# Modulation blocks accumulated on VectorE in the first FFN's loop, and an input projection begun with four feature tiles per chunk of tokens

## What is computed

```
mod = silu(c) @ w_mod + b_mod            # sh1,sc1,g1, sh2,sc2,g2, sh3,sc3,g3
h = rmsnorm(x, ng[0]) * (1 + sc1) + sh1
x = x + g1 * 0.5 * swiglu(h, gate0, up0, down0)        # FFN width 2816
h = rmsnorm(x, ng[1]) * (1 + sc2) + sh2
proj = h @ w_in                          # 2560 columns: q, k, v, xr, xg
o  = differential attention(q, k, v)     # 4 heads
rg = bidirectional RG-LRU(conv(xr)) * gelu(xg)
x = x + g2 * (concat(o, rg) @ w_out)
h = rmsnorm(x, ng[2]) * (1 + sc3) + sh3
x = x + g3 * 0.5 * swiglu(h, gate1, up1, down1)
y = rmsnorm(x, final_g)
```

## Time and profile before

| what | value |
|---|---|
| runs of the kernel before | 2498.46, 2496.99, 2494.31 us; median 2496.99 |
| the profiled execution | 2498.43 us, span 2496.6 us |
| granted TensorE clock, mean over the span | 0.978 of full speed |
| PE, PEld, DVE, ACT, POOL busy | 2396.6, 2236.1, 1128.3, 668.6, 29.7 us |
| DMA | 144.52 MB, mean 58 GB/s |

### The profile page before, as it was taken

One profiled execution on the slowest core, in us unless ns is written; L12 is line 12 of the kernel. 1 busy time (PEld: TensorE's weight loads), 2 busy tenths in 40 slices (PEclk: granted clock), 3 DMA queues, 4 the chain that ended last, 5 costly groups with the idle time before them and its releaser, 6 DMA issues.

```text
span 2496.6 us, 35528 instructions
## 1 busy us (share of the span) xinstructions
PE 2396.6 (96%) x14392; PEld 2236.1 (90%) x14392; DVE 1128.3 (45%) x1845; ACT 668.6 (27%) x1174; POOL 29.7 (1%) x36
## 2 busy tenths in 40 slices
PE   5999999999999998999989988999999999999997
PEld 3799999999999987777977768979999999999996
DVE  3544333443334436465557773364443344443335
ACT  3411111111111124465236663251111111111112
POOL 0000000000000000000010030000000000000000
PEclk8999999999999999999989999999999999999998
DMA  9222022210222103111100010111101110101102
GB/s 372 85 75 77 18 83 84 77 74 20 81 84 82 44 1 119 34 34 41 43 21 20 29 46 18 59 52 34 50 22 46 50 50 34 49 22 46 50 9 77
DMA packets 45817, 144.52 MB, mean 58 GB/s; under 512 B 5808, under 2 KB 13360, under 8 KB 45744
## 3 DMA queue, kind: packets, MB, share of 16 engines
q1 hardware_dynamic: 45744, 143.49, 16.7%
HBM read 133.50 MB, written 9.97 MB: 57 GB/s over the span
## 4 chain that ended last, share of the span: by engine, by line
PE 90%; DVE 4%; ACT 3%; DMA 1%; issue 1%; SPq 0%; ACTq 0%; DVEq 0%
PE ps L433 27%; PE ps L435 26%; PE ps L434 26%; PE ps L679 4%; PE ps L708 2%; PE ps L632 2%; DVE sb_tmp L1191 1%; PE ps L694 1%; DVE sb_hL L1183 1%; PE ps L460 1%; DMA sb_stage<-in_w_mod 1%; ACT sb_pr L1036 1%; PE ps L445 1%; PE ps L453 0%; PE ps L470 0%
## 5 line engine op out<-in xcount | busy, mean ns | idle before, releaser
L433 PE MATMUL ps<-sb_hH,sb_guH 128*128 128x384 f32 x2112 | 716.2, 339 | 9.8 <-DVE sb_hL L1183 6.3
L435 PE MATMUL ps<-sb_hH,sb_guL 128*128 128x384 f32 x2112 | 708.0, 335 | 0.0
L434 PE MATMUL ps<-sb_hL,sb_guH 128*128 128x384 f32 x2112 | 708.0, 335 | 0.0
L433 PEld LDWEIGHTS ps<-sb_hH,sb_guH 128*128 128x128 f32 x2112 | 398.0, 188 | 33.7 <-issue 17.4
L1255 DVE SCALAR_TENSOR_TENSOR sb_x<-ps,sb_mod,sb_x 128x128 f32<-128x128 f32 (+1 forms) x704 | 345.9, 515 | 180.9 <-PE ps L435 178.7
L434 PEld LDWEIGHTS ps<-sb_hL,sb_guH 128*128 128x128 f32 x2112 | 398.4, 189 | 0.7 <-issue 0.3
L435 PEld LDWEIGHTS ps<-sb_hH,sb_guL 128*128 128x128 f32 x2112 | 398.3, 189 | 0.0
L1242 DVE TENSOR_TENSOR sb_tmp<-ps,sb_tmp 128x384 f32<-128x384 f32 x132 | 73.5, 557 | 670.6 <-PE ps L435 669.3
L433 PE MATMUL ps<-sb_hidH,sb_dnH 128*128 128x384 f32 x1056 | 356.4, 338 | 0.5 <-DVE sb_x L1255 0.4
L435 PE MATMUL ps<-sb_hidH,sb_dnL 128*128 128x384 f32 x1056 | 353.2, 334 | 0.0
L434 PE MATMUL ps<-sb_hidL,sb_dnH 128*128 128x384 f32 x1056 | 353.1, 334 | 0.0
(11 more groups left out here) (152 smaller groups left out, 2228.0 us busy)
## 6 DMA issues: line engine op xcount, KB each, us to landing
sb_raw<-in_w_gate SPq DMA_DIRECT2D x44, 512.0 KB, 4.5
sb_raw<-in_w_up SPq DMA_DIRECT2D x44, 512.0 KB, 3.7
sb_raw<-in_w_mod SPq DMA_DIRECT2D x44, 512.0 KB, 4.1
sb_raw<-in_w_down SPq DMA_DIRECT2D x44, 512.0 KB, 4.4
sb_stage<-in_w_mod SPq DMA_DIRECT2D x7, 2048.0 KB, 18.6
sb_raw<-in_w_in SPq DMA_DIRECT2D x16, 512.0 KB, 4.0
sb_x<-in_x SPq DMA_DIRECT2D x3, 1536.0 KB, 10.5
x_spilled<-sb_x SPq DMA_DIRECT2D x8, 576.0 KB, 5.5
```

The lines of the kernel that those rows point to most:

```text
L433: pe.matmul(o, wH, xH, start=begin, stop=False)
L434: pe.matmul(o, wH, xL, start=False, stop=False)
L435: return pe.matmul(o, wL, xH, start=False, stop=end)
```

## The change

Two parts.

**Modulation.** In passes 1 to 10 PE no longer does `mod_partial`, ACT no longer `mod_evac`. DVE multiplies each half of a raw block (128 x 512) by the two conditionings' values, which lie one per partition in `cs`, and accumulates over the four quarters of `w_mod`'s rows and two halves: 16 operations, two accumulators, `modp` and the first half of slot 3. PE then sums over partitions by 8 matmuls with 128 columns of an accumulator as weights and one column of `ones` as data (`ones` holds 1/D, so the result is multiplied by D). These stand after the up product of chunk 2 of the first tile. The passes' order on ACT and DVE for z = 0 is changed, too: the slots of the raw block are now set free by DVE between its other work, slot 3 by PE. Pass 0 is as before.

**Projection.** Four tiles of weights are held at its start (`wjH`, `wjL` for tiles 2 and 3, in memory that `v` uses later), and the order is (0,c) (1,c) (2,c) (3,c) for c = 0, 1, 2. `stats(1, 2)` moves into (3,0), `spread(1, 2)` into (0,1). ACT casts four tiles before the norm, and takes results 0 to 3 out among the `h_hi` of chunk 2. DVE makes two low parts after the adds of chunk 0 and two after those of chunk 1. `conv(0)` now waits for result 8, (0,2), and stands behind the low parts of tiles 4 and 5. The loads of tiles 2 and 3 lie ahead of the copies of `x`.

```diff
+            def mod_collect(i):
+                pe.wait_ge(mod_acc, i * 16)
+                pe.wait_ge(mod_done, i + PRE)
+                for n in range(4):
+                    for cond, src in ((0, raw[:, nth(0, "m3", 0)[0]]), (1, modp[:])):
+                        m = pe.matmul(ps[:, 7, 2 * n + cond:2 * n + cond + 1], src[:, n * P:(n + 1) * P], ones[:, 0:1],
+                                      start=True, stop=True)
+                        if n == 3 and cond == 0:
+                            m.then_inc(raw_used[3], 1)
+                m.then_inc(mod_sum, 1)
...
-                if with_mod:
-                    mod_raw_full(i)
-                    pe.wait_ge(mod_done, i + PRE)
-                    mod_partial(raw, True)
...
-                        if with_mod and f == 0 and c == 0:
-                            pe.wait_ge(mod_copy, i + (PRE + 1))
-                            mod_total()
+                        if with_mod and f == 0 and c == 2:
+                            mod_collect(i)
...
+                def mod_part(n, q):
+                    slot, use = nth(0, f"m{q}", i)
+                    dve.wait_ge(raw_full[slot], use * 16 + 16)
+                    for kk in range(2):
+                        src = raw[:, slot, kk * 512:(kk + 1) * 512]
+                        for cond in (1, 0):
+                            at = 4 * n + 2 * kk + 1 - cond
+                            by = cs[:, 2 * q + kk, cond:cond + 1]
+                            if at < 2:
+                                m = dve.tensor_scalar(sums_at[cond], src, by, None, ALU.mult)
+                            else:
+                                dve.wait_ge(mod_acc, i * 16 + (at - 17))
+                                m = dve.scalar_tensor_tensor(sums_at[cond], src, by, sums_at[cond], ALU.mult, ALU.add)
+                            m.then_inc(mod_acc, 1)
+                    if q < 3:
+                        dve.wait_ge(mod_acc, i * 16 + (4 * n + 4 - 16))
+                        dve.sem_inc(raw_used[slot], 1)
...
             for c in range(NC):
-                for f in range(2):
-                    in_chunk(f, c, 2 * c + f, used_in[f])
-            for e in range(2, 4):
-                for c in range(NC):
-                    in_chunk(e, c, e * NC + c, e // 2 + used_in[e % 2])
+                for e in range(4):
+                    in_chunk(e, c, 4 * c + e, used_in[e])
...
-                    elif (e, c) == (0, 1):
+                    elif (e, c) == (3, 0):
                         stats(1, 2, (k,))
-                    elif (e, c, k) == (1, 1, 4):
+                    elif (e, c, k) == (0, 1, 4):
                         spread(1, 2)
...
+            def first_evac(o):
+                in_evac(xr[:, o % 4, chunk(o // 4)], o)
+                if o in (8, 9):
+                    cast(wiH[:, o % 4], o % 4, used_in[o % 4] + 1)
...
-            for e in range(2, 4):
+            for e in range(4, 6):
                 lo(wiL[:, e % 2], e % 2, None, wiH[:, e % 2], whi_in + e + 1)
             dve.wait_ge(spilled, 16 * KT)
             conv(0)
-            for e in range(4, 6):
-                lo(wiL[:, e % 2], e % 2, None, wiH[:, e % 2], whi_in + e + 1)
```

More of the change, by code:

```diff
@@ L845, in norm @@
                 if z < 3:
-                    h_hi(z, NC - 1)
+                    for k in range(KT):
+                        h_hi(z, NC - 1, (k,))
+                        if between is not None:
+                            between(k)
             def mod_evac(b, used):
@@ L898, in gu1, with down @@
                     cast(guH[1][:, j].rearrange("p k n -> p (k n)"), *nth(z, "gu"[j] + "1", i), (s["u"], i * 6 + 6))
[L900 to L906, removed]
+                def down(j):
+                    cast(dnH[:, j], *nth(z, f"d{j}", i), (s["d"], i * 24 + 24))
+                if not with_mod:
                     hidden(0, 0)
@@ L911, in ffn_act @@
                     gu1(1)
-                for j in range(2):
-                    cast(dnH[:, j], *nth(z, f"d{j}", i), (s["d"], i * 24 + 24))
-                if with_mod:
+                    down(0)
+                    down(1)
+                elif z == 0:
+                    gu1(0)
+                    hidden(0, 0)
+                    gu1(1)
+                    hidden(0, 1)
+                    down(0)
+                    down(1)
+                else:
+                    gu1(0)
+                    gu1(1)
+                    hidden(0, 0)
+                    down(0)
+                    down(1)
                     hidden(0, 1)
@@ L929, in _ @@
             act.wait_ge(ffn[0]["u"], 6 + NG * 6)
-            for e in range(2):
-                cast(wiH[:, e], e, used_in[e])
-            norm(1, lambda c, k: (ffn[0]["x"], 3 + (NG - 1) * 24 + c * KT + k + 1))
+            for e in range(4):
+                cast((wiH, wjH)[e // 2][:, e % 2], e, used_in[e])
             def in_evac(dst, o):
@@ L937, in in_evac @@
                 act.activation(dst, ps[:, o % 6, 0:CH], ACT.Copy).then_inc(m_ev, 1)
-            for c in range(NC):
-                for f in range(2):
-                    in_evac(xr[:, f, chunk(c)], 2 * c + f)
-            for e in range(2, 4):
[L943 to L947, removed]
+            def first_evac(o):
+                in_evac(xr[:, o % 4, chunk(o // 4)], o)
+                if o in (8, 9):
+                    cast(wiH[:, o % 4], o % 4, used_in[o % 4] + 1)
+            norm(1, lambda c, k: (ffn[0]["x"], 3 + (NG - 1) * 24 + c * KT + k + 1),
+                 lambda k: first_evac(k // 2) if k % 2 else None)
+            for o in range(4, 12):
+                first_evac(o)
             def v_evac(n):
@@ L1275, in ffn_dve @@
                     mod_add(PRE)
-                for j in range(2):
-                    weights(dnL[:, j], dnH[:, j], f"d{j}", j + 3)
-                if with_mod:
+                    down(0)
+                    down(1)
+                elif z == 0:
+                    mod_part(0, 3)
+                    gu1(0)
+                    mod_part(1, 0)
+                    mod_part(2, 1)
+                    hidden(0, 0)
+                    mod_part(3, 2)
+                    gu1(1)
+                    hidden(0, 1)
+                    down(0)
+                    down(1)
+                else:
+                    gu1(0)
+                    gu1(1)
+                    hidden(0, 0)
+                    down(0)
+                    down(1)
                     hidden(0, 1)
```

70 lines of the change are left out of this document (40 added, 30 removed).

## The result

| | before | changed | forecast |
|---|---|---|---|
| runs, median | 2497.59 us (4, 2494.31 to 2498.46) | 2477.40 us (4, 2473.26 to 2478.63) | 2475.0 us |
| ratio, 95% interval | | 0.9918 [0.9904, 0.9931] | 0.9912 |
| profiled execution | 2498.43 us, span 2496.6 | 2477.22 us, span 2475.5 | 2476.4 us |
| pass of the first FFN's loop | 77.83 us | 76.67 us | 76.6 |
| (0,0) to the third gate product | 71.43 us | 60.59 us | 60.55 |

A forecast was written before the change was run, and what follows sets the result against it. PE was taken as the bound, holding 90% of the chain. Savings of 12.5 us (modulation) and 9.5 us (projection) sum to 22.0 us off 2498.4, giving 2476.4; with the runs' median 1.4 us lower, 2475.0 us, range 2470 to 2485.

The forecast's parts named there:

- What leaves PE and what comes: In passes 1 to 10, PE loses 2.96 us and gains 1.71 us, saving 1.25 us per pass, 12.5 us in all.
- Weight loads: In `mod_collect`, loads go on under running matmuls, so 16 steps cost 0.101 us each, not the 0.19 us load.
- the first rival: In `mod_collect`, weight loads don't overlap and cost 0.19 us each: 2 us worse over ten passes, 2489.5 us; chance 0.07.
- DVE's load and the slack: In a pass, 16 operations of 0.74 us; `hidden(0, 0)` runs at 10.7 us, PE wants it at 20.8.
- The third rival: In the loop, DVE bounds a pass; from 1.51 us per operation it outweighs both savings; 2527 us at 1.7; chance 0.04.
- The norm: Before the projection, DVE makes two low parts instead of one, so (0,0) begins 1.14 us later.
- The projection: From the projection's start to the gates, PE's waits go; the third gate product comes 9.5 us earlier, range 7 to 11.5.
- The second rival: At `conv(0)`, late chunk 2 of h delays tile 4's load; part two gains 4.5 us, time 2480; chance 0.15.
- From the gates on the order is as before, so nothing gives the time back: Behind the projection, the order is unchanged, so the 9.5 us gained there are kept.

The follow-up runs named there:

- experiment 5: The changed kernel with the matmuls of `mod_collect` made twice, 32 in place of 16 in passes 1 to 10: 2501.64 us, ratio 1.0015.
- part one alone: The kernel before with only the modulation of passes 1 to 10 changed, the projection as it was: 2485.79 us, ratio 0.9952.
- experiments 6: The changed kernel with 8 more 128x512 operations on DVE at the start of passes 1 to 10: 2472.53 us, ratio 0.9906.
- 7: The changed kernel with 16 more 128x512 operations on DVE at the start of passes 1 to 10: 2491.50 us, ratio 0.9980.
- second trace of the changed kernel: The changed kernel run once more, unaltered, on the chip of the first follow-up runs: 2476.69 us, ratio 0.9913.
- part two alone: The kernel before with only the projection's start changed, the modulation loop as it was: 2483.32 us, ratio 0.9944.
- 8: The changed kernel with two low parts moved behind the norm's reciprocal and tile 0's convolution ahead of tile 5's low part: 2476.09 us, ratio 0.9914.
- 9: The changed kernel with 8 more 128x384 matmuls, overwritten behind them, ahead of (3,2): 2472.68 us in one execution.
- 10: The changed kernel with 16 more 128x384 matmuls, overwritten behind them, ahead of (3,2): 2478.82 us in one execution.

## Why the prediction was right

- **What leaves PE and what comes** was 1.25 us per pass, measured 1.16. The term that was off is the step of a matmul of `mod_collect`: 0.101 us from the two-column matmuls of the earlier trace rows, 0.112 by the starts of the pairs and by experiment 5 (78.46 - 76.67 for 16 more). It lies between the bounds given, 0.101 and 0.12. Ten passes: 11.6 us for 12.5.
- **Weight loads.** 16 loads of 128x128 and their matmuls went by in 1.7 us where 0.19 each would be 3.04, and part one alone brought 12.0 us. So the price of the first rival did not come. The Trainium skill (TensorE: Matmul & The Clock Gate, Part 3, "The mechanism") says that a weight load overlaps matmuls in flight only where it goes to another row group. Against that rule the 1.7 us prove less than the prediction took them for: 0.19 us is the length of a load's record, and in the stream of 128x384 matmuls such loads start 0.17 apart, so the record is longer than the time for which a load keeps the next one waiting. A load that took 0.11 us and overlapped nothing would fit the step of 0.112, too. The stream speaks against the rule more clearly: at the half clock of 1.2 GHz a 128x384 matmul with its own full load takes 0.32 us from start to start (experiment 5), which is 384 cycles for 384 columns and leaves no time for a load, unless more than one column goes in a cycle. How much of a load runs under a one-column matmul stays open; the sum needs only the step.
- **DVE's load and the slack** held in size and place: 0.75 us per operation, `hidden(0, 0)` at 10.1, and experiments 6 and 7 show PE waiting for `hidden(0, 0)` about where the 20.8 us put it. The third rival, DVE as the bound, needed 1.51 us an operation.
- **The norm** was to come 1.14 us later for the second low part. From the first `mod_collect` to (0,0) the changed kernel takes 757.81 us and part one alone (0,0 at 933.14, first `mod_collect` at 176.27) 756.87: 0.94 us.
- **The projection** was forecast from (0,0) to the third gate product as 60.55 us and took 60.59. The single steps of its trace fit within 0.4 us: (2,0) begins 10.66 us behind (0,0) (forecast 10.66), (0,1) at 22.92 (23.25), (0,2) at 40.37 (40.75). That the sum fits to 0.04 is luck: in the second trace of the changed kernel the half-clock stretch at (0,0) lasts longer, and it takes 59.65 us to the table load instead of 58.66. The second rival did not come about: the convolution starts at 987.14, 51.5 us behind (0,0), where 1005.4 - 5.98 - 947.55 = 51.9 was forecast.
- **"From the gates on the order is as before, so nothing gives the time back"** is the step that failed, without showing in the total. The gates brought 2.9 us more, and 3.4 us were lost later, at unchanged work. That the two nearly cancel is luck: with one of them alone the time would have been some 3 us off the measured one, about 2474 or 2480, both still in the range of 2470 to 2485. With part two alone the loss is missing and 3.1 us more are gained ahead of the third norm, and it brings 14 us instead of 9.5. The two parts alone sum to 26.0 us, together they bring 20 (on the spans of single executions 12.6 + 15.0 against 21.1); the intervals are too wide to tell these sums apart by themselves, the stretches of the traces show where the difference lies. Stretches of the same code between gates(2) and the third norm take 520.1 to 526.4 us over the twelve traces, and 525.2 and 526.4 in the two of the changed kernel alone. A sum for this kernel is therefore not good to better than some 3 us, whatever the digits of its terms.

## What to carry to other kernels

Where PE is full and DVE idle for half of the time, work may be moved even at a bad rate: here 10.1 us of DVE bought 1.16 us of PE per pass. What such a move needs is the time at which PE wants DVE's next product, and an experiment that loads DVE on purpose measures this slack better than any busy share. For a gain of 1 to 3 us around pauses of PE, look at the granted clock of both traces stretch by stretch before it is put down to an order of instructions, and take a second trace of each kernel.

## What was not expected of the hardware

- **The clock decides microseconds at unchanged work.** A gate stage has 192 matmuls. The windows of the stage from gates(1), before and changed:

```profile
1053.64:1091.35 37.71, 35.62 (x192) 27.99 (x192) 26.12 (x25) 22.48 (x30) 0.00 (x0) 0.95 0.00 1
```

```profile
1030.56:1066.83 36.27, 34.14 (x192) 27.41 (x192) 26.13 (x25) 22.48 (x30) 0.00 (x0) 1.00 0.00 1
```

The 1.44 us are one stretch of about 3.4 us at 1.2 GHz behind the pause. Behind gates(0) it stood in all three traces with the old projection, where the pause was 1.98 us, and in none of the nine with the new one, where it is 1.39 or 1.40; whether the shorter pause is the reason was not tried by itself. Behind gates(1), with 1.98 us in all, it is missing in six traces with the new projection (the changed kernel twice, experiments 2, 5, 6 and 7) and there in three (8 to 10). It was the same in both executions of the kernel before and in both of the changed one, and it changes with a shift of a few us ahead of it, so it is hardly plain chance and not a property of the work. The traces say one thing more on the moment. The clock was at half around the start of (0,0) in all twelve, too, and came back to full at some time behind it:

```profile
935.72:939.13 3.41, 3.41 (x10) 3.23 (x11) 1.46 (x3) 0.34 (x1) 0.00 (x0) 0.50 0.92 358
```

```profile
935.40:938.80 3.40, 3.09 (x16) 2.82 (x17) 2.17 (x5) 0.60 (x2) 0.00 (x0) 0.50 0.71 280
...
1034.37:1037.79 3.42, 3.42 (x14) 1.05 (x12) 0.47 (x1) 1.74 (x3) 0.00 (x0) 0.50 0.00 0
```

These are windows of the changed kernel and of the one with 8 fillers. Counted from there (939.13 in the first) the pause of gates(1) begins 90.4 to 91.4 us later in the six traces without the half-clock stretch, and 89.8, 92.7 and 92.5 us later in the three with it (experiments 8, 9 and 10). Counted from the start of the span it begins between 1028.7 and 1056.1 us in the six, and between 1029.5 and 1033.1 in the three. So the place of the pause against the clock's own last change separates the nine, and its place in the span does not. This was found in the traces afterwards; no run was made to test it. Why it should decide stays open, and so does the loss of 1.2 us around the third norm (of the 1.99 in the table) and 1.4 in the second FFN: it stands in both traces of the changed kernel and in experiments 8 and 10, not in 1, 2, 5, 6, 7 and 9.
- **A run of one-column matmuls can drop the clock although PE never waits**: 32 of them (3.46 us) did in four of ten passes, at 9.5 us, 16 of them (1.7 us) in no pass of any trace.
